# Expert weights laid out in DRAM as the kernel fetches them, two transfers of 2 MB a pass in place of four of 1 MB

## The reference, cut to what matters

```python
def grouped_moe(h, router_w, router_b, w_gate, w_up, w_down):
    ...
    combine = jnp.einsum('nk,nke->ne', top_w, jax.nn.one_hot(top_idx, N_EXPERTS, dtype=jnp.float32))
    y = jnp.zeros((t.shape[0], D), jnp.float32)
    for e in range(N_EXPERTS):
        he = jax.nn.silu(t @ w_gate[e]) * (t @ w_up[e])
        y = y + combine[:, e:e + 1] * (he @ w_down[e]).astype(jnp.float32)
    return y.reshape(B_, S, D).astype(h.dtype)
```

## Time and profile before

| what | value |
| --- | --- |
| median of three runs | 2042.43 us |
| the three runs | 2041.69, 2042.43, 2044.41 us |
| span of the profiled execution | 2041.6 us |
| instructions | 32610 |
| PE busy | 1897.6 us (93%) |
| DVE busy | 1175.1 us (58%) |
| ACT busy | 943.9 us (46%) |
| POOL busy | 77.4 us (4%) |
| DMA moved | 476.43 MB, mean 233 GB/s |
| expert loads | 192 of 1024 KB |
| first and second mixture-of-experts stage, TensorE's passes | 244.1 to 503.2 us, 666.1 to 922.1 us |

### The profile page before, as it was taken

One profiled execution on the slowest core, in us unless ns is written; L12 is line 12 of the kernel. 1 busy time (PEld: TensorE's weight loads), 2 busy tenths in 40 slices (PEclk: granted clock), 3 DMA queues, 4 the chain that ended last, 5 costly groups with the idle time before them and its releaser, 6 DMA issues.

```text
span 2041.6 us, 32610 instructions
## 1 busy us (share of the span) xinstructions
PE 1897.6 (93%) x13784; PEld 1381.8 (68%) x13784; DVE 1175.1 (58%) x1636; ACT 943.9 (46%) x1347; POOL 77.4 (4%) x132
## 2 busy tenths in 40 slices
PE   6998988798998988889999998899999999999998
PEld 4787523244976332338888987788887888778887
DVE  5778633444877432447556664665556675636565
ACT  4345445345463543455445733354445444445442
POOL 2031000000010000000000000000000000200000
PEclk9999999989999989899999989999999999999999
DMA  9887999998958899995555410255555555605552
GB/s 357 320 263 264 333 387 386 387 368 292 344 164 318 310 387 387 371 339 196 186 189 178 127 44 4 85 185 188 195 179 175 192 195 186 171 1 191 195 192 104
DMA packets 261218, 476.43 MB, mean 233 GB/s; under 512 B 8513, under 2 KB 118145, under 8 KB 255697
## 3 DMA queue, kind: packets, MB, share of 16 engines
q1 hardware_dynamic: 250960, 431.02, 60.6%
q0 software_dynamic: 10112, 43.32, 6.4%
HBM read 472.17 MB, written 2.14 MB: 232 GB/s over the span
## 4 chain that ended last, share of the span: by engine, by line
PE 73%; DMA 12%; DVE 7%; ACT 5%; issue 2%; SPq 0%; POOL 0%; ACTq 0%; DVEq 0%; POOLq 0%
PE psum L1175 16%; PE psum L1210 11%; PE psum L1616 9%; PE psum L1180 8%; PE psum L1130 6%; DMA experts<-in_exp_w_down 4%; DMA experts<-in_exp_w_up 4%; DMA experts<-in_exp_w_gate 2%; PE psum L1558 1%; PE psum L1344 1%; PE psum L1079 1%; PE psum L1143 1%; PE psum L1145 1%; PE psum L1144 1%; DVE w_lo L3112 1%
## 5 line engine op out<-in xcount | busy, mean ns | idle before, releaser
L3112 DVE TENSOR_TENSOR w_lo<-ring,w_hi 128x2048 fp32r<-128x2048 f32 x191 | 436.0, 2289 | 192.2 <-ACT w_hi L2344 190.4
L2344 ACT ACTIVATE w_hi<-ring 128x2048 fp32r<-128x2048 f32 x191 | 364.7, 1913 | 207.0 <-PE psum L1210 118.1
L1175 PE MATMUL psum<-h_both,w_hi 128*128 128x512 f32 x1408 | 442.6, 395 | 1.9 <-DVE h_both L3894 1.3
L1180 PEld LDWEIGHTS psum<-h_both,w_lo 128*128 128x128 f32 x1408 | 264.5, 188 | 61.8
L2550 ACT ACTIVATE pool<-experts 128x512 f32 x332 | 184.0, 621 | 228.1 <-PE psum L1616 98.0
L3552 DVE COPY pool<-experts 128x512 f32 x380 | 140.9, 423 | 245.2 <-PE psum L1616 115.4
L1180 PE MATMUL psum<-h_both,w_lo 128*128 128x256 f32 x1408 | 277.3, 278 | 0.0
L1175 PEld LDWEIGHTS psum<-h_both,w_hi 128*128 128x128 f32 x1408 | 217.4, 189 | 5.7 <-issue 1.7
L2376 ACT ACTIVATE pool<-psum 128x512 f32<-128x512 f32 x88 | 52.6, 598 | 254.6 <-PE psum L1180 254.5
L1616 PE MATMUL psum<-pool 128*32 128x512 f32 x1008 | 128.4, 626 | 12.5 <-DVE pool L3552 8.5
L1616 PE MATMUL psum<-experts,pool 128*32 128x512 f32 x1024 | 122.3, 607 | 15.7 <-DMA experts<-in_exp_w_down 12.9
(11 more groups left out here) (507 smaller groups left out, 2998.6 us busy)
## 6 DMA issues: line engine op xcount, KB each, us to landing
experts<-in_exp_w_gate SPq DMA_DIRECT2D x64, 1024.0 KB, 12.1
experts<-in_exp_w_up SPq DMA_DIRECT2D x64, 1024.0 KB, 14.4
experts<-in_exp_w_down SPq DMA_DIRECT2D x64, 1024.0 KB, 15.0
ring<-in_ffn_pre_w_in SPq DMA_DIRECT2D x44, 1024.0 KB, 5.1
ring<-in_ffn_post_w_in SPq DMA_DIRECT2D x44, 1024.0 KB, 5.2
ring<-in_ada_w SPq DMA_DIRECT2D x24, 1024.0 KB, 7.0
ring<-in_ffn_pre_w_out SPq DMA_DIRECT2D x22, 1024.0 KB, 4.9
ring<-in_ffn_post_w_out SPq DMA_DIRECT2D x22, 1024.0 KB, 4.9
```

What stands on the lines that cost most here:

```text
L1175: pe.matmul(bank(4 + 2 * j + f).rearrange("p (s n) -> p s n", s=2), wh[:, k, P * f:P * f + P], h_both[:, :, k, :], start=k == 0, stop=Fals ...
L1180: return pe.matmul(bank(4 + 2 * j + f)[:, 0:T], wl[:, k, P * f:P * f + P], h_hi[:, k, :], start=False, stop=k == KD - 1, skip_group_check= ...
L2344: act.activation(w_hi[:, (s["split"] + r) % 3, :], piece(s["pieces"][r]), ACT.Copy)\
L3112: dve.tensor_tensor(w_lo[:, slot, :], piece(s["pieces"][r]), w_hi[:, slot, :].bitcast(F32), ALU.subtract).then_inc(sem("w_lo"), 1)
```

## The change

On the host, the three expert inputs are put together into one array `exp_blocks` of shape (2 layers, 24 passes, 2 halves, 128 partitions, 4096): for each pass and each half of the experts the 2 MB stand in a row, with the 16 KB of a partition together. SP's `load_blocks` fetches one half with one transfer. It takes the waits of both blocks that it fills, or for a refill the later of their `m_base` values; the first twelve blocks become six loads, and in the first stage the last two of them are no longer in the order block 3, 0, 1, 2. The landing of two neighbouring base groups is now told by one semaphore, `m_landed` with the pass modulo 3 and g // 2. TensorE, VectorE and ScalarE run the same instructions.

```diff
--- before.py
+++ after.py
@@ -556,7 +556,7 @@
             return ("m_base", BASE_GROUPS * n + g + 1) if g < BASE_GROUPS else ("m_over", 4 * n + g - 3)
 
         def pass_landed(layer, p, g):
-            return f"m_landed{p % MOE_DEPTH}{g}", 16 * (MOE_PASSES // MOE_DEPTH * layer + p // MOE_DEPTH + 1)
+            return f"m_landed{p % MOE_DEPTH}{g // 2}", 16 * (MOE_PASSES // MOE_DEPTH * layer + p // MOE_DEPTH + 1)
 
         hid = [view(WORK + 4096, 2, HC), view(WORK + 4608, 2, HC)]
         up_sum = [hT[:, 0:2, :], hT[:, 2:4, :]]
@@ -783,40 +783,32 @@
             def moe(name, blocks):
 
                 layer = int(name[-1])
-                def load_block(p, g):
-
-                    kind, k = kind_of(p)
-                    es = slice(4 * g, 4 * g + 4)
-                    if kind == "down":
-                        h, f = k // 4, k % 4
-                        src = a["exp_w_down"][layer, es, P * f:P * f + P, 512 * h:512 * h + 512]
-                    else:
-                        src = a["exp_w_gate" if kind == "gate" else "exp_w_up"][layer, es, P * k:P * k + P, :]
-                    at = 512 * (NE * third(layer, p) + 4 * g)
-                    sp.dma_start(experts[:, at:at + 4 * 512].rearrange("p (e n) -> p e n", e=4), src.rearrange("e p n -> p e n"))\
-                      .then_inc(sem(pass_landed(layer, p, g)[0]), 16)
-
-                order = [(p, g) for p in range(MOE_DEPTH) for g in range(BASE_GROUPS)]
-                if layer == 0:
-                    order[8:12] = [(2, 3), (2, 0), (2, 1), (2, 2)]
-                for p, g in order:
-                    block = BASE_GROUPS * third(layer, p) + g
-                    if block >= 3:
-                        for e in blocks[block - 3]:
-                            sp.wait_ge(sem(e[0]), e[1])
-                    elif layer == 0:
-                        sp.wait_ge(sem("ada1_used"), (12, 14, 16)[block])
-                    elif block == 0:
-                        sp.wait_ge(sem("sb_pv"), 16)
-                    load_block(p, g)
+                def load_blocks(p, half):
+
+                    at = 512 * (NE * third(layer, p) + 8 * half)
+                    sp.dma_start(experts[:, at:at + 8 * 512], a["exp_blocks"][layer, p, half])\
+                      .then_inc(sem(pass_landed(layer, p, 2 * half)[0]), 16)
+
+                for p in range(MOE_DEPTH):
+                    for half in range(2):
+                        for g in (2 * half, 2 * half + 1):
+                            block = BASE_GROUPS * third(layer, p) + g
+                            if block >= 3:
+                                for e in blocks[block - 3]:
+                                    sp.wait_ge(sem(e[0]), e[1])
+                            elif layer == 0:
+                                sp.wait_ge(sem("ada1_used"), (12, 14, 16)[block])
+                            elif block == 0:
+                                sp.wait_ge(sem("sb_pv"), 16)
+                        load_blocks(p, half)
                 for p in range(MOE_DEPTH, MOE_PASSES):
                     n = MOE_PASSES * layer + p
-                    for g in range(BASE_GROUPS):
-                        sp.wait_ge(sem("m_base"), BASE_GROUPS * (n - MOE_DEPTH) + g + 1)
-                        if g == 0:
+                    for half in range(2):
+                        sp.wait_ge(sem("m_base"), BASE_GROUPS * (n - MOE_DEPTH) + 2 * half + 2)
+                        if half == 0:
                             sp.wait_ge(sem("m_dve"), len(DVE_TILES) * (n - MOE_DEPTH + 1))
                             sp.wait_ge(sem("m_act"), len(ACT_TILES) * (n - MOE_DEPTH + 1))
-                        load_block(p, g)
+                        load_blocks(p, half)
 
             for n, pc in enumerate(PL.pieces):
                 if pc["kind"] == "moe":
@@ -3935,8 +3927,15 @@
             swiglu("post1")
 
 
-_WEIGHTS = ["x", "c", "ada_w", "ada_b", "even_w_in", "even_w_out", "odd_w_in", "odd_w_out", "router_w", "exp_w_gate",
-            "exp_w_up", "exp_w_down", "mem_2", "ffn_pre_w_in_2", "ffn_pre_w_out_2", "ffn_post_w_in_2",
+def expert_blocks(gate, up, down):
+
+    by_row = [w.reshape(2, 2, 8, KD, P, 512).transpose(0, 3, 1, 4, 2, 5) for w in (gate, up)]
+    by_half = down.reshape(2, 2, 8, 4, P, 2, 512).transpose(0, 5, 3, 1, 4, 2, 6)
+    return np.concatenate([w.reshape(2, 8, 2, P, 2 * PIECE) for w in (*by_row, by_half)], 1)
+
+
+_WEIGHTS = ["x", "c", "ada_w", "ada_b", "even_w_in", "even_w_out", "odd_w_in", "odd_w_out", "router_w",
+            "mem_2", "ffn_pre_w_in_2", "ffn_pre_w_out_2", "ffn_post_w_in_2",
             "ffn_post_w_out_2", "mem_w_kv_2", "a_w_in_2", "a_w_up_2", "a_a_up_2", "a_g_up_2", "a_w_out_2", "b_w_q_2",
             "b_w_out_2", "kv_w_2", "rel_bias_2", "a_lnx_g_2", "a_lnx_b_2", "router_b"]
 
@@ -3965,6 +3964,7 @@
          n["mem_k_norm_2"].reshape(-1), n["b_q_norm_2"].reshape(-1), n["kv_k_norm_2"].reshape(-1)]))
     rel = n["att_rel_bias"][0].T
     arrays["rel_t"] = np.ascontiguousarray(np.concatenate([rel, np.zeros((256 - rel.shape[0], 8), rel.dtype)], 0))
+    arrays["exp_blocks"] = expert_blocks(n["exp_w_gate"], n["exp_w_up"], n["exp_w_down"])
     arrays.update(constants())
 
     nc = _bacc.Bacc("TRN2", target_bir_lowering=False, num_devices=1)
```

## The result

The changed kernel takes **2009.43 us** (median of four runs, 2007.13 to 2018.40), against 2042.97 us of the kernel before beside it (four runs). The ratio is 0.9843, 95% interval 0.9820 to 0.9867: 1.6%, 32 us by the ratio and 33.5 by the medians. Five later runs (e4) gave 0.9831 (0.9810 to 0.9851). The forecast was 2005 with a range of 1993 to 2020. The profiled execution took 2011.06 us with a span of 2009.3 us.

The account below looks back on a forecast made before the run. DMA was taken to set the steady-state pace in the expert stages, 3.3 us a pass over TensorE, though not everywhere. Terms -20.2 (first stage), -17.5 (second) and +1 (POOL's loads) gave -36.7 from 2042.4, said as 2005 us, range 1993 to 2020.

Parts of the forecast that it names:

- 84 refills by 0.24 us, the packet line: First-stage expert refills: time per packet is 37.5 ns per KB plus 14 ns, so 2.71 becomes 2.47 us per MB, -20.2 us.
- Slow spots: Eight places in the down passes at 311 to 344 GB/s vanish with the new layout: -4.3 and -4.0 us.
- Coarser waits: Pass 23, group 2 waits for the second half: +3.3 us ending the first stage, 3.8 in the second; pass 19 absorbed.
- First stage: Whether TensorE keeps up there: last landing 465.4, nearly balanced with TensorE, stage end 482.9, -20.2 us.
- Second stage: Refills from pass 6 on run at the queue's rate: last landing 887.5, end 904.6, -17.5 us including 3.8 for the coarser wait.
- Neighbours: POOL's modulation-weight loads lose queue share beside 16 KB packets: about +1 us at 626.5 to 633.2, ends 0 and +4.
- A chain through POOL's loads longer by over 4 us: Sign of being wrong: the chain of waits through POOL's loads grows by more than 4 us.
- SP's issues: SP issues 48 loads a stage and not 96; issue was held back by a full queue, so 0 us.
- smaller fixed cost: Rival: a packet's fixed cost is smaller, 2.60 us a MB, 403 GB/s, 2022 us; chance 0.09 with other partial gains.
- nothing changes in rate: Rival: runs are cut back into small packets, or 387 GB/s is the memory's limit; 2042 us, chance 0.04.
- reads collide: Rival: engines walking 16 KB rows collide in memory, 3.30 us a MB, 2134 us; chance 0.05.
- More than forecast: Rival: fewer TensorE waits could spare some time at the lower clock; -43 to -56 us, 1986 to 1999, chance 0.10.

Follow-up runs that it names:

- e4: The changed kernel run once more, unaltered, in a later call: 2012.01 us, ratio 0.9831 to the kernel before.
- e3: The kernel before, with only the down weights laid out as two arrays of 512 columns, still 2 KB packets: 2037.33 us, ratio 0.9966.
- e6: The changed kernel, but in passes 19 and 23 the second half comes as two 1 MB loads and group 2 waits for the first alone: 2008.79 us.
- e1: The change's 2 MB transfers and waits, with the weights left in DRAM as in the kernel before, in 2 KB runs: 2059.87 us, ratio 1.0073.
- e5: The changed kernel with two more waits on SP's queue, holding one expert load in each stage until POOL's load has landed: 2000.00 us.

## Why the prediction was right

It was right in sign and size, and in its main mechanism; one term failed, and in another the size came out by a path that was not the one forecast. By its numbered terms, and in its order:

1. *84 refills by 0.24 us, the packet line.* Right: 427 GB/s measured against 425 taken, 4.9 us from one 2 MB landing to the next. The fixed time of a packet is better read as 9 ns than as my 14: the 104.9% of the earlier trace rows count an overlap of the 2 KB packets. I carried the overlap into the 89 ns, and at 16 KB it makes no difference.
2. *Slow spots.* Right that they go, and why (e3). The size 8.3 us stands against 7 by e3's time.
3. *Coarser waits, +3.3 and +3.8.* Mixed. With the changed rate, pass 23 of the first stage waits 1.69 us for them in one execution, and in e6 nothing is gained there; in the second stage the cost is in pass 19, which I had said the buffer would absorb, and not in pass 23, where TensorE reaches group 2 at 875.5, behind the last landing at 873.8. Where the wait was there at all, the executions differ: 1 to 6 us in pass 19 (told above). At the old rate (e1) they cost more than I priced.
4. *First stage.* Forecast -20.2, measured -21.4 (e4: -18.4). Counted from the first pass, the last landing came at the forecast 465.4 (472.5 less the 7.1 us by which that pass started later), and the end at 481.8 for 482.9.
5. *Second stage.* Forecast -17.5, measured -18.5 (e4: -16.8). The agreement is partly luck. I had the stage end on the last landing, at 887.5 with a coarser wait of 3.8 us behind it. Counted from the stage's own start, which is 11.2 us earlier than before, the landing came at 885.0, and TensorE was behind it; what it had lost on the way, in pass 19 above all, took the place of my term.
6. *Neighbours.* **The step that failed**: "in the first stage one load 3 us later and the next ones level", priced at nothing. The load is 4.2 us longer, and the row that the working left out, TensorE's wait of 0.57 us for VectorE behind it, says how little of that is covered. Together with 1.4 us for this and the next products at the lower clock (1.94 for 1.06, and 1.22 for 0.70) it makes the +5.0, which e5 takes back. A chain through POOL's loads longer by over 4 us was one of the prediction's own signs of being wrong, and it came. Between the stages I said +1, with an end of +4; measured +3.1, 2.9 of it by the time that POOL's load has landed. The upper end of that bound was the better value. "The experts' own load passes sooner" did not help enough: the 2 MB expert load issued 1.5 us ahead of POOL's (610.9) lands only 0.6 us before it, at 621.1, and no other one was in flight then, the next being issued at 625.4.
7. *SP's issues.* Nothing showed of it.

The sum: forecast -36.7, measured -32.3 between the spans. The difference of 4.4 is, up to rounding, +5.0 in front of the first stage, +2.1 more between them, -2.2 in the stages, and outside the changed part +2.1 early and -2.7 late, which are spread. Those two nearly cancel, and that they do is luck. Because of the late starts the two stages end 14 and 30 us earlier, counted from the start of the span, and not about 20 and 37. Of the rivals, "smaller fixed cost", "nothing changes in rate" and "reads collide" are all answered by the 427 GB/s. "More than forecast" did not come as such.

## What to carry to other kernels

Where a queue of loads is never empty, as here, the length of the run that one partition reads set the rate (387 to 427 GB/s), and the order of the weights in DRAM is the knob: 8 KB has nearly all of it, and larger transfers alone gave nothing. Longer runs also took share from the one other queue that was busy, one packet for one packet; before lengthening them, list the loads of other queues in flight beside them, and the slack of each at the engine that waits for it. And price a coarser wait at the rate after the change: it costs where TensorE is waiting for data, and nothing where it is late itself.

## What the runs showed of the hardware

**The spread of the changed kernel goes with TensorE's clock.** Its nine runs go from 2002.2 to 2019.2 us, and the mean granted clock from 0.988 to 0.975, nearly in step (the three slowest have 0.975, 0.975 and 0.978, the fastest 0.988); a straight line through them is 1.15 us for each thousandth. What the clock is in a stretch differs between executions of the same code: from pass 7 to pass 8 of the second stage TensorE takes 18.2 us in the changed kernel, at 0.91, and 23.5 us in e4, the same kernel, at 0.67. In e3 the lower clock between 316 and 328 us goes with a pass 8 that starts some 5 us late. What makes one execution get the lower clock there and another not, no run here shows. A change worth 3 us is told by its place in the trace, if at all, and not by the medians.

**Sixteen busy engines at 290 to 318 GB/s by address alone.** The same 2 KB packets in the same order give 378 to 387 GB/s once the down halves lie apart, as e3 shows against the earlier trace rows and e1. Which banks or channels collide, no run here shows, and why only the experts 8 to 15 were struck was not tried.
